# Other start addresses in SBUF for the weight buffers and for the arrays that stream past them

## The chip, the cores and the metric

The kernel runs on one core of one Trainium2 chip. The metric is device time in microseconds (us) of one execution; a kernel's time is the median of its runs.

## The reference

A first block (rms norm, one wide projection, chunked attention with relative bias, a short convolution, two gated branches, a mixture of 32 experts in 4 groups, a gated per-token embedding), then a second block of two layers on 512 tokens and 16 meta tokens: a pooling mixer and a SwiGLU FFN in layer 0, sliding-window attention and a SwiGLU FFN in layer 1.

```python
z = n @ w_in[i] + b_in[i]
...
m = jax.nn.sigmoid(ga) * (ya @ w_pa[i]) + jax.nn.sigmoid(gc) * (yc @ w_pc[i])
h = h + m @ w_o[i]
...
hdn = jax.nn.silu(xb @ w1[e]) * (xb @ w3[e])
return hdn @ w2[e]
...
gate = jax.nn.sigmoid(rms_norm(h, g_ple[i]) @ w_ple_gate[i] + b_ple_gate[i])
h = h + gate * (p[i] @ w_ple_proj[i])
...
gu = h @ w_gate_up
gate, up = jnp.split(gu, 2, axis=-1)
return (jax.nn.silu(gate) * up) @ w_down
```

All data are float32, D = 1024, S = 512 tokens, L = 528 with the meta tokens, and the FFN is 2816 wide.

## The kernel before

Activations lie transposed: 128 features on the partitions, tokens along the free axis, one row per block of 128 features. Every dense product outside the experts is made of three matmuls in float32r, since each operand is held as a high and a low part: high weights on high data, high weights on low data, low weights on high data. The helper `tile` (its matmul is L484) makes one output block: for each of the K blocks of 128 input features it issues, for each range of tokens, the three matmuls into one PSUM bank. The weights are the stationary operand (128 by 128); the tokens' row is the moving one and streams past them:

```python
for o, c0, c1 in outs:
    for n, (a, x) in enumerate(((wh, hi), (wh, lo), (wl, hi))):
        i = e.matmul(o, a, x[:, k0 + k, c0:c1], start=(k == 0 and n == 0),
                     stop=(k == j.K - 1 and n == 2))
```

Each matmul has a weight load (LDWEIGHTS, the row PEld) of its own. Of S-wide arrays (xhi, mhi, yahi, ychi, n1hi, g1hi, qhi and their low parts) a row is 512 tokens, streamed whole or in halves of 256. Of L-wide ones (nhi, nlo, ghi, glo, all of layer 0) a row is 528 tokens, streamed as 272 and 256. L1134 and L878 are the same three matmuls written out for the openings of the two FFNs, where several output blocks take turns with each row; L540 makes the values of the first attention with x as the stationary operand and the weights streamed.

Weights come in units of 8 blocks, 128 x 1024 in float32. SP loads a unit into one of four `raw` buffers, ScalarE casts it into a high part `whi` (L2319), VectorE takes the difference as the low part `wlo` (L1318), and PE waits for it by the event "lo". There are four places for such pairs (0 to 3), and four more (4 to 7) and again four (8 to 11, named wh8 to wh11 and wl8 to wl11) in stretches where room is free. `wslot(u)` names the place of unit u.

The experts (L700 up, L724 down, L735 and L736 to spread the result over the tokens) use plain float32 weights out of ten slots `e0` to `e9` of 16 KB per partition, which SP loads one after another from about 350 to 850 us.

The addresses are set by hand: a `Place` hands out addresses one after another, rounded to 32 bytes, and may be started anywhere. `keep` holds what lives throughout; behind it stand three regions of 49152 bytes, EB (raw, whi, wlo), EA and EC (activations), and XR. The function `like_weights(o)` (L303) raises an address until it has the weights' residue modulo 256; it sets n1hi, n1lo, g1hi, g1lo, and osum, qhi, qlo. The order of the work is the order in which each engine's program is written; addresses have no part in it.

Of the kernel before, what the change touches and what calls it, by code (L numbers as in the profile page):

```python
# [7 lines left out]
F32R = mybir.dt.float32r  # L8
# [6 lines left out]
S = 512  # L15
MT = 16
L = S + MT
# [121 lines left out]
def build_program(nc, T, out, known):  # L139
    with ExitStack() as ctx:  # L140
        marks = Marks(nc, ctx, known)
        _program(nc, ctx, T, out, marks)
        return marks.now


def _program(nc, ctx, T, out, marks):
# [5 lines left out]
    class Place:  # L152
# [3 lines left out]
        def __call__(self, name, shape, dt=F32):  # L156
            t = nc.alloc_sbuf_tensor_at(name, shape, dt, offset=self.off)
            self.off += (4 * int(np.prod(shape[1:])) + 31) // 32 * 32
            return t

    keep = Place(nc.sbuf_base)
    hT = keep("hT", [128, 8, L])
    cst = keep("cst", [128, NCST])
# [14 lines left out]
    ove = keep("ove", [128, 16], I32)  # L178
    wr = Place(dg_at)("wr", [128, 8, 36])
    rr = Place(dg_at)("rr", [128, 2, 3, 68])  # L180
    EB, EA, EC = keep.off, keep.off + 49152, keep.off + 98304
    XR = keep.off + 147456
    ident, ones, tri = cst[:, 0:128], cst[:, 128:256], cst[:, 256:384]
    half, tokid = cst[:, 384:512], cst[:, 512:516]

    pl = Place(EB)
# [9 lines left out]
    pl = Place(EA)  # L196
# [8 lines left out]
    pl = Place(EC)  # L205
# [3 lines left out]
    yalo = pl("yalo", [128, 4, S], F32R)  # L209
    pl = Place(XR)  # L210
    ychi = pl("ychi", [128, 4, S], F32R)
# [4 lines left out]
    Bt.append(pl("B1", [128, 2, S]))  # L216
    pl = Place(XR)
    mhi = pl("mhi", [128, 8, S], F32R)
    mlo = pl("mlo", [128, 8, S], F32R)
    sg = pl("sg", [128, 2, S])  # L220

    LAST = (nc.sbuf_usable_end - 16384) // 32 * 32
    slots = [Place(o + 16384 * i)(f"e{c}", [128, 4096]) for c, (o, i) in enumerate(
        ((EA, 1), (EA, 2), (EA, 0), (EC, 0), (EC, 1), (EC, 2), (EB, 0), (EB, 1), (EB, 2), (LAST, 0)))]
    WIDE = 50
# [20 lines left out]

    pl = Place(XR)
    xg = [pl("xg0", [128, D])]
    pl.off = XR + 4160
    xg.append(pl("xg1", [128, D]))  # L250
# [7 lines left out]
    pick = pl("pick", [128, S], F32R)  # L258
    assert pl.off <= LAST
    pl = Place(XR)  # L260
    pick_last = pl("pick15", [128, S], F32R)
    h2 += [pl(f"h2{i}", [128, 4, C]) for i in (2, 3)]
    assert pl.off <= XR + 4160

# [16 lines left out]
    pl = Place(EB + 8192)  # L281
    pThi = pl("pThi", [128, 2, S], F32R)
    pTlo = pl("pTlo", [128, 2, S], F32R)
    pl = Place(XR)
# [3 lines left out]
    pl = Place(EA)  # L288
# [2 lines left out]
    zacc = pl("zacc", [128, L])  # L291
    zq = [pl(f"zq{i}", [128, 272]) for i in range(5)]
    tmp = [pl(f"ztmp{i}", [128, 272]) for i in range(3)]
    y_at = pl.off
    yT = pl("yT", [128, 8, L])
    f_at = pl.off
    ghi = pl("ghi", [128, 12, L], F32R)
    glo = pl("glo", [128, 12, L], F32R)
    sl = [pl(f"sl{i}", [128, L]) for i in range(2)]
    gdiag = pl("gdiag", [128, 8, 128])  # L300
    assert pl.off <= nc.sbuf_usable_end

    def like_weights(o):  # L303
        return o + (EB - o) % 256

    n1hi = Place(like_weights(EA))("n1hi", [128, 8, S], F32R)
    n1lo = Place(like_weights(EA + 32 * L))("n1lo", [128, 8, S], F32R)
    g1hi = Place(like_weights(f_at))("g1hi", [128, 12, S], F32R)
    g1lo = Place(like_weights(f_at + 48 * L))("g1lo", [128, 12, S], F32R)
    assert like_weights(EA + 32 * L) + 32 * S <= EA + 64 * L  # L310
    assert like_weights(f_at + 48 * L) + 48 * S <= f_at + 96 * L
    assert like_weights(f_at) + 48 * S <= f_at + 48 * L
    ho = Place(EA)("ho", [128, 4, D])
    XW = 4
    whi += [None] * 8
# [1 line left out]
    pl = Place(f_at)  # L317
# [6 lines left out]
    plo = [None, pl("plo1", [128, 8, 256], F32R)]  # L324
    pl.off = max(pl.off, (LAST - 13824) // 32 * 32)
    assert pl.off >= f_at + 96 * L + 8 * L
    zn = pl("zn", [128, 8, MT + 272])
    ws = [pl(f"ws{i}", [128, 2, 14 + 272]) for i in range(2)]
    assert pl.off <= LAST
    pl = Place(LAST)  # L330
    pp = [pl(f"pp{i}", [128, 8, 256]) for i in range(2)]
    pl = Place(y_at)
    phi[0] = pl("phi0", [128, 8, 256], F32R)
    plo[0] = pl("plo0", [128, 8, 256], F32R)
    for n, (x, o) in enumerate(((whi, f_at + 4 * 4 * L), (wlo, f_at + 16 * 4 * L))):
        pl = Place(o)
# [4 lines left out]
    pl = Place(f_at)  # L341
# [3 lines left out]
    B2 = [pl(f"B2{i}", [128, 4, 256]) for i in range(2)]  # L345
    PT2 = [pl(f"PT2{i}", [128, 4, 128]) for i in range(2)]
    sm = pl("sm", [128, 5, 64])
    pl.off = like_weights(pl.off + 32 * S)
    osum = Place(pl.off)("osum", [128, 8, S])
    qhi = pl("qhi", [128, 8, S], F32R)  # L350
    qlo = pl("qlo", [128, 8, S], F32R)
# [2971 lines left out]
```

## Time and profile before

| | us |
|---|---|
| median of 3 runs | 1949.69 |
| all runs | 1949.5, 1949.69, 1953.39 |
| profiled execution, its time and its span | 1949.5 |
| PE busy | 1888.2 |
| VectorE busy | 917.4 |
| ScalarE busy | 637.3 |
| GpSimd busy | 139.6 |

The profile is of one execution, the one of 1949.5 us. PE's busy time is made of modelled ends, and successive matmuls overlap in it: a matmul's own duration in a row (some 0.39 us for 512 columns) holds the way through the array, and the time from one start to the next is what a stream of them costs. DMA moves 345.16 MB in the span.

### The profile page before, as it was taken

Reading aid. Unit: us, or ns where it says so; the run is one execution under the profiler, and the core shown is the slowest. Engines: PE = TensorE matmul, PEld = TensorE weight load, DVE = VectorE, ACT = ScalarE, POOL = GpSimd, SP = SyncE. Lnnn points to the kernel's source line nnn. Section 1 sums busy time; section 2 is a strip of 40 time slices with the busy share of each in tenths; the row PEclk is TensorE's granted clock in tenths of the full one; section 3 lists DMA queues with packets and bytes.
Section 4 is the critical chain, followed back from the end, with each engine's and each line's share of the span. In section 5 each row is a group of like instructions: output and inputs, shape, how many; then the busy total and the mean of one; then the engine's idle time right before and its main releaser. Section 6 shows DMA issues by size and latency. Waiting matters only on the chain.

```text
span 1949.5 us, 31374 instructions
## 1 busy us (share of the span) xinstructions
PE 1888.2 (97%) x13564; PEld 1563.9 (80%) x13564; DVE 917.4 (47%) x1611; ACT 637.3 (33%) x1187; POOL 139.6 (7%) x120
## 2 busy tenths in 40 slices
PE   7999999999999999999899999999999999999998
PEld 5866788866666666669789999999867898888898
DVE  5755334233332333247873322347866574423355
ACT  6344323121111011126532222234466543222242
POOL 0022000110000000000000000004222100000011
PEclk9999999999999999999899999999999999999999
DMA  5222242689999999973112332334321213332343
GB/s 190 87 76 76 86 170 94 267 348 427 425 425 426 423 427 424 426 291 91 47 61 83 91 98 78 96 104 144 111 66 55 79 53 108 94 110 82 104 126 112
DMA packets 57149, 345.16 MB, mean 177 GB/s; under 512 B 7168, under 2 KB 7808, under 8 KB 44976
## 3 DMA queue, kind: packets, MB, share of 16 engines
q1 hardware_dynamic: 53184, 334.15, 46.4%
q0 software_dynamic: 3504, 8.54, 1.3%
q8 instruction: 108, 1.77, 0.4%
q10 hardware_dynamic: 320, 0.43, 0.1%
q14 instruction: 33, 0.27, 0.0%
HBM read 343.09 MB, written 4.19 MB: 178 GB/s over the span
## 4 chain that ended last, share of the span: by engine, by line
PE 84%; DVE 7%; DMA 6%; ACT 1%; issue 1%; POOL 0%; SPq 0%; DVEq 0%; ACTq 0%; POOLq 0%
PE bank L484 57%; PE bank L700 8%; PE bank L724 6%; DMA e<-in_we 6%; PE bank L735 1%; PE bank L540 1%; PE bank L736 1%; DVE wlo L1318 1%; PE bank L1134 1%; PE bank L1081 1%; PE bank L917 1%; PE bank L1053 1%; PE bank L878 1%; PE bank L687 1%; PE bank L557 1%
## 5 line engine op out<-in xcount | busy, mean ns | idle before, releaser
L1318 DVE TENSOR_TENSOR wlo<-raw,whi 128x1024 fp32r<-128x1024 f32 x230 | 286.6, 1253 | 127.3 <-ACT whi L2319 123.3
L2319 ACT CAST whi<-raw 128x1024 fp32r<-128x1024 f32 x231 | 239.8, 1043 | 127.3 <-PE bank L484 110.3
L700 PE MATMUL bank<-e,xT 128*64 128x256 f32 x2048 | 234.7, 382 | 1.0 <-DVE xT L1591 1.0
L700 PEld LDWEIGHTS bank<-e,xT 128*64 128x64 f32 x2048 | 143.0, 137 | 80.5 <-issue 11.2
L484 PE MATMUL bank<-nhi,whi 128*128 128x272 f32 (+1 forms) x672 | 191.6, 285 | 1.1 <-DVE sl L1847 0.6
L484 PE MATMUL bank<-nhi,wlo 128*128 128x272 f32 (+1 forms) x672 | 191.2, 285 | 0.0
L484 PE MATMUL bank<-nlo,whi 128*128 128x272 f32 (+1 forms) x672 | 190.6, 284 | 0.0
L484 PE MATMUL bank<-n1hi,whi 128*128 128x512 f32 (+1 forms) x448 | 163.0, 364 | 0.0
L484 PE MATMUL bank<-n1hi,wlo 128*128 128x512 f32 (+1 forms) x448 | 160.8, 359 | 0.0
L484 PE MATMUL bank<-n1lo,whi 128*128 128x512 f32 (+1 forms) x448 | 160.8, 359 | 0.0
L724 PE MATMUL bank<-e,h 128*64 128x256 f32 x1024 | 118.7, 392 | 11.7 <-DMA e<-in_we 11.2
L484 PEld LDWEIGHTS bank<-nhi,whi 128*128 128x128 f32 x672 | 127.2, 189 | 2.0 <-DVE sl L1847 0.8
L484 PEld LDWEIGHTS bank<-nlo,whi 128*128 128x128 f32 x672 | 126.8, 189 | 0.0
L484 PEld LDWEIGHTS bank<-nhi,wlo 128*128 128x128 f32 x672 | 126.3, 188 | 0.0
L1618 DVE SCALAR_TENSOR_TENSOR ylo<-bank,tcol,yhi 128x512 fp32r<-128x512 f32 x32 | 24.0, 751 | 211.4 <-ACT yhi L2500 211.4
L484 PE MATMUL bank<-xhi,whi 128*128 128x512 f32 x288 | 121.2, 421 | 1.3 <-DVE xlo L1342 1.3
L724 PEld LDWEIGHTS bank<-e,h 128*64 128x64 f32 x1024 | 79.2, 141 | 49.2 <-issue 15.3
L484 PE MATMUL bank<-xhi,wlo 128*128 128x512 f32 x288 | 112.8, 392 | 0.0
L484 PE MATMUL bank<-xlo,whi 128*128 128x512 f32 x288 | 112.5, 391 | 0.0
L484 PE MATMUL bank<-ghi,whi 128*128 128x272 f32 (+1 forms) x352 | 101.3, 288 | 2.8 <-DVE wlo L1318 2.7
L484 PE MATMUL bank<-ghi,wlo 128*128 128x272 f32 (+1 forms) x352 | 100.7, 286 | 0.0
L484 PE MATMUL bank<-glo,whi 128*128 128x272 f32 (+1 forms) x352 | 100.5, 285 | 0.0
(397 smaller groups left out, 3762.9 us busy)
## 6 DMA issues: line engine op xcount, KB each, us to landing
e<-in_we SPq DMA_DIRECT2D x94, 2048.0 KB, 22.6
raw<-in_w_down SPq DMA_DIRECT2D x64, 512.0 KB, 3.6
raw<-in_w_gate SPq DMA_DIRECT2D x44, 512.0 KB, 3.6
raw<-in_w_up SPq DMA_DIRECT2D x44, 512.0 KB, 3.6
raw<-in_w_q SPq DMA_DIRECT2D x12, 512.0 KB, 4.5
B<-in_rel POOLq DMA_DIRECT2D x8, 512.0 KB, 4.7
raw<-in_w_gc SPq DMA_DIRECT2D x8, 512.0 KB, 3.5
raw<-in_w_ga SPq DMA_DIRECT2D x8, 512.0 KB, 4.3
```

Of the source, the lines that this page charges most:

```text
L484: i = e.matmul(o, a, x[:, k0 + k, c0:c1], start=(k == 0 and n == 0), stop=(k == j.K - 1 and n == 2))
L540: p = e.matmul(bs[i][:, 0:256], x[:, k, t], a, start=(k == 0 and n == 0), stop=(k == 7 and n == 2))
L557: e.matmul(b[:, 0:n], qk[pb:pb + 64, hp, t * 128:(t + 1) * 128], qk[pb:pb + 64, 4 + hp, 0:n], start=True, stop=True).then_inc(*hit("pe_att ...
L687: i = e.transpose(b[:, k * 128:(k + 1) * 128], xg[0 if ov else p % 2][:, (4 * c + k) * 128:(4 * c + k + 1) * 128], ident)
L700: p = e.matmul(b[64 * hf:64 * hf + 64, 0:256], x[:, k, :], W[:, k, 256 * hf:256 * hf + 256], start=(k == 0), stop=(k == 7))
L724: i = e.matmul(b[64 * x:64 * x + 64, 256 * q:256 * q + 256], h2_of(2 * p + x)[:, 2 * (kc % 2) + kc // 2, :], W[x][:, kc, 512 * nh + 256 * ...
L735: e.matmul(b[:], yhi[:, k * 128:(k + 1) * 128], pick_of(p)[:], start=True, stop=False)
L736: e.matmul(b[:], ylo[:, k * 128:(k + 1) * 128], pick_of(p)[:], start=False, stop=True).then_inc(*hit(f"pe_moe{ov}", ("spread y", p, k)))
L878: p = e.matmul(o, a, x[:, k, c0:c1], start=(k == 0 and n == 0), stop=(k == 7 and n == 2))
L1318: e.tensor_tensor(wlo[wslot(u)][:], raw[u % NRAW][:], whi[wslot(u)][:].bitcast(F32), ALU.subtract).then_inc(*hit("dve_low", ("lo", u)))
L1618: e.scalar_tensor_tensor(ylo[:, c], bk("y", p, nh), tcol[:, 1, p:p + 1], yhi[:, c].bitcast(F32), ALU.mult, ALU.subtract).then_inc(*hit(f"d ...
L2319: e.copy(whi[wslot(u)][:], raw[u % NRAW][:]).then_inc(*hit("act_high", ("hi", u)))
```

## The change

Only addresses change. EB is put 64 bytes past a multiple of 256, EA and with it EC and XR at multiples of 256; `like_weights` gives way to `whole`, which rounds up to 256; the last slot `LAST`, yT and what starts there are put at multiples of 256, and f_at (ghi, glo, and the places 4 to 11) 64 past one. No instruction, wait or transfer is added, dropped or moved to another point of its engine's order.

The residues modulo 256 that come out, with the relation, which is the stationary operand's start less the moving one's, modulo 256:

| stationary / streamed | before | relation | after | relation |
|---|---|---|---|---|
| places 0 to 3 / xhi, mhi, yahi, ychi, n1hi, g1hi, qhi and low parts | 96 / 96 | 0 | 64 / 0 | 64 |
| places 0 to 3 / pThi, pTlo | 96 / 96 | 0 | 64 / 64 | 0 |
| places 0 to 3 / phi0, plo0 | 96 / 160 | 192 | 64 / 0 | 64 |
| places 0 to 3 / phi1, plo1 | 96 / 160 | 192 | 64 / 64 | 0 |
| places 4 to 7 / phi0, plo0 | 160 / 160 | 0 | 64 / 0 | 64 |
| places 4 to 7 / phi1, plo1 | 160 / 160 | 0 | 64 / 64 | 0 |
| places 8 to 11 / n1hi, n1lo | 160 / 96 | 64 | 64 / 0 | 64 |
| xhi, xlo / places 0 to 3 (L540) | 96 / 96 | 0 | 0 / 64 | 192 |
| yhi, ylo / pick (L735, L736) | 160 / 160 | 0 | 64 / 64 | 0 |
| places 0 to 3 / rows of nhi, ghi | 96 / 32, 96, 160, 224 | all four | 64 / 0, 64, 128, 192 | all four |
| experts' slots e0 to e8; e9 (DMA targets) | 96; 224 | | 0 or 64; 0 | |

```diff
--- before.py
+++ after.py
@@ -157,6 +157,9 @@
             t = nc.alloc_sbuf_tensor_at(name, shape, dt, offset=self.off)
             self.off += (4 * int(np.prod(shape[1:])) + 31) // 32 * 32
             return t
+
+    def whole(o):
+        return (o + 255) // 256 * 256
 
     keep = Place(nc.sbuf_base)
     hT = keep("hT", [128, 8, L])
@@ -178,8 +181,9 @@
     ove = keep("ove", [128, 16], I32)
     wr = Place(dg_at)("wr", [128, 8, 36])
     rr = Place(dg_at)("rr", [128, 2, 3, 68])
-    EB, EA, EC = keep.off, keep.off + 49152, keep.off + 98304
-    XR = keep.off + 147456
+    EB = whole(keep.off) + 64
+    EA = whole(EB + 49152)
+    EC, XR = EA + 49152, EA + 98304
     ident, ones, tri = cst[:, 0:128], cst[:, 128:256], cst[:, 256:384]
     half, tokid = cst[:, 384:512], cst[:, 512:516]
 
@@ -219,7 +223,7 @@
     mlo = pl("mlo", [128, 8, S], F32R)
     sg = pl("sg", [128, 2, S])
 
-    LAST = (nc.sbuf_usable_end - 16384) // 32 * 32
+    LAST = (nc.sbuf_usable_end - 16384) // 256 * 256
     slots = [Place(o + 16384 * i)(f"e{c}", [128, 4096]) for c, (o, i) in enumerate(
         ((EA, 1), (EA, 2), (EA, 0), (EC, 0), (EC, 1), (EC, 2), (EB, 0), (EB, 1), (EB, 2), (LAST, 0)))]
     WIDE = 50
@@ -291,25 +295,22 @@
     zacc = pl("zacc", [128, L])
     zq = [pl(f"zq{i}", [128, 272]) for i in range(5)]
     tmp = [pl(f"ztmp{i}", [128, 272]) for i in range(3)]
-    y_at = pl.off
+    y_at = pl.off = whole(pl.off)
     yT = pl("yT", [128, 8, L])
-    f_at = pl.off
+    f_at = pl.off = whole(pl.off) + 64
     ghi = pl("ghi", [128, 12, L], F32R)
     glo = pl("glo", [128, 12, L], F32R)
     sl = [pl(f"sl{i}", [128, L]) for i in range(2)]
     gdiag = pl("gdiag", [128, 8, 128])
     assert pl.off <= nc.sbuf_usable_end
 
-    def like_weights(o):
-        return o + (EB - o) % 256
-
-    n1hi = Place(like_weights(EA))("n1hi", [128, 8, S], F32R)
-    n1lo = Place(like_weights(EA + 32 * L))("n1lo", [128, 8, S], F32R)
-    g1hi = Place(like_weights(f_at))("g1hi", [128, 12, S], F32R)
-    g1lo = Place(like_weights(f_at + 48 * L))("g1lo", [128, 12, S], F32R)
-    assert like_weights(EA + 32 * L) + 32 * S <= EA + 64 * L
-    assert like_weights(f_at + 48 * L) + 48 * S <= f_at + 96 * L
-    assert like_weights(f_at) + 48 * S <= f_at + 48 * L
+    n1hi = Place(whole(EA))("n1hi", [128, 8, S], F32R)
+    n1lo = Place(whole(EA + 32 * L))("n1lo", [128, 8, S], F32R)
+    g1hi = Place(whole(f_at))("g1hi", [128, 12, S], F32R)
+    g1lo = Place(whole(f_at + 48 * L))("g1lo", [128, 12, S], F32R)
+    assert whole(EA + 32 * L) + 32 * S <= EA + 64 * L
+    assert whole(f_at + 48 * L) + 48 * S <= f_at + 96 * L
+    assert whole(f_at) + 48 * S <= f_at + 48 * L
     ho = Place(EA)("ho", [128, 4, D])
     XW = 4
     whi += [None] * 8
@@ -345,7 +346,7 @@
     B2 = [pl(f"B2{i}", [128, 4, 256]) for i in range(2)]
     PT2 = [pl(f"PT2{i}", [128, 4, 128]) for i in range(2)]
     sm = pl("sm", [128, 5, 64])
-    pl.off = like_weights(pl.off + 32 * S)
+    pl.off = whole(pl.off + 32 * S)
     osum = Place(pl.off)("osum", [128, 8, S])
     qhi = pl("qhi", [128, 8, S], F32R)
     qlo = pl("qlo", [128, 8, S], F32R)
```

## Rows read from the trace of the kernel before

**Rows 1.** The page: span, busy time by engine, TensorE's clock in 40 slices.

```profile
span 1949.5 us, 31374 instructions
...
PE 1888.2 (97%) x13564; PEld 1563.9 (80%) x13564; DVE 917.4 (47%) x1611; ACT 637.3 (33%) x1187; POOL 139.6 (7%) x120
...
PEclk9999999999999999999899999999999999999999
```

**Rows 2.** The page: the chain that ended last, by line.

```profile
PE bank L484 57%; PE bank L700 8%; PE bank L724 6%; DMA e<-in_we 6%; PE bank L735 1%; PE bank L540 1%; PE bank L736 1%; DVE wlo L1318 1%; PE bank L1134 1%; PE bank L1081 1%; PE bank L917 1%; PE bank L1053 1%; PE bank L878 1%; PE bank L687 1%; PE bank L557 1%
```

**Rows 3.** The longest of PE's waits: total us, times, longest us.

```profile
PE bank L724 <- DMA e<-in_we: 11.2, 5, 4.3
```

**Rows 4.** Window 350 to 850 us: busy by engine, PEclk, DMA share, GB/s.

```profile
350.00:850.00 500.00, 483.47 (x3757) 329.49 (x3758) 155.59 (x300) 64.39 (x131) 25.88 (x24) 0.98 0.97 403
```

**Rows 5.** Timeline of PE from 1660 us (start, us, what), first and last.

```profile
1659.66 0.39 PE L484 MATMUL bank<-n1hi,wlo 128*128 128x512 f32 x1
...
1661.47 0.39 PE L484 MATMUL bank<-n1lo,whi 128*128 128x512 f32 x1
```

**Rows 6.** Timeline of PE from 1545 us, first and last.

```profile
1545.43 0.28 PE L484 MATMUL bank<-n1hi,whi 128*128 128x256 f32 x1
...
1546.39 0.28 PE L484 MATMUL bank<-n1hi,wlo 128*128 128x256 f32 x1
```

**Rows 7.** Timeline of PE from 1598 us, places 8 to 11 at L484.

```profile
1597.83 0.28 PE L484 MATMUL bank<-n1hi,wl 128*128 128x256 f32 x1
...
1598.96 0.28 PE L484 MATMUL bank<-n1hi,wh 128*128 128x256 f32 x1
```

**Rows 8.** Timeline of PE, from 1566 us, L1134, places 8 to 10.

```profile
1565.73 0.28 PE L1134 MATMUL bank<-n1lo,wh 128*128 128x256 f32 x1
...
1567.14 0.28 PE L1134 MATMUL bank<-n1lo,wh 128*128 128x256 f32 x1
```

**Rows 9.** Timeline of PE from 918 us, phi1 with places 0 to 3.

```profile
918.43 0.28 PE L484 MATMUL bank<-plo,whi 128*128 128x256 f32 x1
...
919.84 0.28 PE L484 MATMUL bank<-plo,whi 128*128 128x256 f32 x1
```

**Rows 10.** Lines by form, PE: first products of 512 columns at L484.

```profile
L484 PE MATMUL bank<-n1hi,whi 128*128 128x512 f32 x320 | 125.8, 393 | 0.0
...
L484 PE MATMUL bank<-xhi,whi 128*128 128x512 f32 x288 | 121.2, 421 | 1.3 <-DVE xlo L1342 1.3
...
L484 PE MATMUL bank<-g1hi,whi 128*128 128x512 f32 x96 | 37.3, 389 | 0.0
...
L484 PE MATMUL bank<-pThi,whi 128*128 128x512 f32 x16 | 6.7, 417 | 0.0
```

**Rows 11.** Lines by form, PE: first products, 256; L-wide ones (page).

```profile
L484 PE MATMUL bank<-g1hi,whi 128*128 128x256 f32 x160 | 46.2, 289 | 0.0
...
L484 PE MATMUL bank<-phi,whi 128*128 128x256 f32 x128 | 37.9, 296 | 0.0
...
L484 PE MATMUL bank<-n1hi,whi 128*128 128x256 f32 x128 | 37.3, 291 | 0.0
...
L484 PE MATMUL bank<-nhi,whi 128*128 128x272 f32 (+1 forms) x672 | 191.6, 285 | 1.1 <-DVE sl L1847 0.6
...
L484 PE MATMUL bank<-ghi,whi 128*128 128x272 f32 (+1 forms) x352 | 101.3, 288 | 2.8 <-DVE wlo L1318 2.7
```

**Rows 12.** Windows of PE: length, busy (matmuls), PEclk, DMA share, GB/s.

```profile
1030.00:1100.00 70.00, 70.00 (x579) 1.00 0.30 91
1640.00:1700.00 60.00, 60.00 (x266) 1.00 0.33 103
```

**Rows 13.** The page: the split of a weight unit on DVE.

```profile
L1318 DVE TENSOR_TENSOR wlo<-raw,whi 128x1024 fp32r<-128x1024 f32 x230 | 286.6, 1253 | 127.3 <-ACT whi L2319 123.3
```

**Rows 14.** Timeline of PE from 353.8 us, on mhi.

```profile
353.89 0.40 PE L484 MATMUL bank<-mhi,wlo 128*128 128x512 f32 x1
...
355.05 0.39 PE L484 MATMUL bank<-mlo,whi 128*128 128x512 f32 x1
```

## The prediction

> **What bounds the kernel now.** The page first. Its span is 1949.5 us, and TensorE (PE) is busy for 1888.2 us of it with the granted clock at 9 tenths or more in all 40 slices but one; VectorE has 917.4 us and ScalarE 637.3 us [rows 1]. In the chain that ended last the one matmul line L484 holds 57% of the span [rows 2]. The waits say the same from the other side: the most that PE spends on anybody is 11.2 us, on the experts' weights [rows 3]. So outside the experts' stage PE never stands still, and what a matmul takes from its own start to the next one's start is the price that counts. Inside that stage the 16 DMA engines are 97% busy [rows 4]; there a faster matmul buys nothing.
>
> The profiled execution (1949.5 us) is the lowest of the three runs and 0.2 us under their median of 1949.69, so sums against it hold for the median.
>
> **How long a matmul really takes.** The column "mean ns of one" holds the pipeline's latency, so I read starts in the timeline. A 512-column matmul on n1hi, n1lo: 1659.66 to 1661.47 is 8 steps, 226 ns each [rows 5]. At 2.4 GHz (PEclk is 1.00 there [rows 12], the higher of its two levels) 512 columns stream in 213.3 ns, so about 13 ns are lost. A 256-column one on the same arrays: 1545.43 to 1546.39, 8 steps, 120 ns against 106.7 for the columns, again 13.3 lost [rows 6]. Whatever the width, the same loss: 32 column times per matmul. In both, the weights' place and the streamed row begin at the same residue, 96 of 256 (the table of residues above).
>
> The kernel before has two places where they do not. At the second half of the last FFN's opening the weights stand in places 8 to 11 (residue 160) while n1 is at 96: weights 64 bytes ahead, which is the relation that the change gives to nearly all S-wide arrays. At L484 the steps there are 1597.83 to 1598.96, 10 of them, 113 ns: 6.6 lost, half of what it was [rows 7]. At L1134, where three places take turns, 1565.73 to 1567.14 is 12 steps of 117.5 ns: 10.8 lost [rows 8]. Weights 64 bytes behind, phi1 at 160 and places 0 to 3 at 96, give 1.41 us for 12 steps, 117.5 ns [rows 9]. So the relation matters, by 2.2 to 6.7 ns a matmul, and equal residues are the worst of the three seen.
>
> **The change, term by term.** No instruction, wait or queue entry is added, dropped or moved; only addresses are. So the sum is a count times a difference in step.
>
> 1. 512-column matmuls at L484 whose relation goes from 0 to 64. There are eight groups of first products there, from n1hi's 320, xhi's 288 and g1hi's 96 down to pThi's 16, 912 in all [rows 10]; each has two sister groups of equal count (the low part streamed, the low part as weights), so 2736. The pThi group stays at relation 0 (64 and 64), which takes off 48: 2688. No row shows 512 columns at relation 64. The loss at relation 0 is the same 13 ns for both widths, so I carry over the two values seen at 256 columns, 6.7 and 2.2 ns gained; the same relation shows both [rows 7, 8] and I take the middle, 4.5: 2688 x 4.5 = 12.1 us. Ends: 5.9 and 18.0 us.
> 2. 256-column matmuls on n1 and g1 at relation 0: (128 + 160) x 3 = 864 [rows 11], x 4.5 = 3.9 us. Ends 1.9 and 5.8.
> 3. phi (128 x 3 [rows 11]): before, half at relation 0 and half at weights-behind; after, phi0 at 64, phi1 at 0. 13.3 and 11.1 become 8.9 and 13.3: 384 x 1.1 = 0.4 us. The values' product (L540, 192 of 256 columns), where weights and stream change roles, goes from 0 to weights-behind: 192 x 2.2 = 0.4 us.
> 4. The L-wide arrays (nhi, nlo, ghi, glo; 3 x 672 + 3 x 352 matmuls [rows 11], with the 288 of layer 0's opening 3360). A row of 528 elements is 2112 bytes, 64 more than a multiple of 256, so the rows walk through all four relations, before as after. They took 70 us for 579 matmuls in the window 1030 to 1100, 120.9 ns at a mean width of 264 columns (110.0 ns), 10.9 lost [rows 12]: the average of the relations. Set at 0; it returns in the rival below.
> 5. The experts' matmuls and the spread of their result (L735, L736, relation 0 before and, but for the last pair, after) lie under the DMA stage. The loads there land at residue 0 or 64 in place of 96 or 224. Nothing in the trace varies that; set at 0, bounded by the 1% or so that 5 us of that stage is, both ways.
> 6. VectorE and ScalarE read and write the moved tiles. One unit of weights is split in 1253 ns [rows 13]; PE needs 24 x 120 = 2.88 us for a unit at 256 columns, 2.77 after. A split grown by half would still hide. Set at 0.
>
> Sum: 12.1 + 3.9 + 0.4 + 0.4 = 16.8 us; 1949.5 - 16.8 = 1932.7, say 1933 us. With terms 1 to 3 at their ends, 1941 to 1925.
>
> **A rule for full speed.** The rows above show 226 ns for 512 columns, never less [rows 5]. The Trainium skill, "TensorE: Matmul & The Clock Gate", section "Wait — 56ns, not 53.3ns?", has back-to-back matmuls at N / 2.4 GHz plus about 2.5 ns, 215.7 ns at N = 512. By that rule, if the new places reached it, the 2688 wide ones alone would give some 29 us, against the 12.1 us of my sum. No run here shows that step.
>
> **Rivals.**
> - *The odd 32 bytes cost too.* Every loss in the trace is near a multiple of 16 columns, or a third of one: 6.7, 11, 13.3. Sixteen columns of four bytes are 64 bytes, and every streamed row of before begins at 32 past a multiple of 64 (residues 32, 96, 160, 224). If memory is read by 64 bytes, each row touches one piece more than it needs, which is 16 columns or 6.7 ns, also in the L-wide arrays. After the change all begin at multiples of 64. For: no stretch in [rows 5 to 9] loses less than 6.6, whatever the relation. Against: no row has an even place to compare. Price: 2736 + 864 + 384 + 192 + 192 (L1134 and its tiles) + 3360 = 7728 matmuls x 6.7 = 51.5 us on top of the 16.8, 1881 us; should only half of it come, 1907.
> - *Nothing changes.* If the losses come from which places follow each other (three in turn at L1134, places 8 to 11), and not from residues, the new ones keep 226 and 120: 1949.5. Against it stand [rows 7, 8] beside [rows 6]: same width and arrays, 20 and 50 us later. The Trainium skill speaks for it: "SBUF — State Buffer", section "Who interferes with whom", gives PE two independent read ports, one for the moving operand and one for the weights, so their places would not meet; by that rule the time is 1949.5 us, and the 120 against 113 of this trace is hard to square with it.
> - *Slower: 512 columns fall into a worse rhythm.* The loss is a standing pattern between two streams, and a wide matmul lets the weights' load meet it elsewhere. A wide pattern worse than 226 exists: 353.89 to 355.05 on mhi is 5 steps of 232 ns [rows 14]. If relation 64 puts the 2688 wide ones there, they lose 5 ns each, 13.4 us, while terms 2 and 3 still gain 4.7: 1958 us. It decides once the wide step is more than (4.7 + 3.9) / 2688 = 3.2 ns over 226.
>
> **Chances.** About 0.2%, 3.9 us, is what a measurement of this kernel can tell from no change. My forecast 0.40; the odd 32 bytes 0.29; nothing 0.14; slower 0.17. The first two are faster: 0.69, the third is same, 0.14, the last slower, 0.17. The range takes in the forecast, most of the 64-byte case and nearly all of the slower one: 1886 to 1958 us. The forecast's own range is 1925 to 1941.
>
> **What would show it.** In the layer-1 FFN (from about 1600 us) the 512-column steps should be 220 to 225 ns and the 256-column ones 113 to 118; the window of L-wide matmuls should still hold 579 in 70 us, while some 610 (114 ns each) would show the 64-byte case. The experts' stage should keep its length and its 97%. Wide steps of 226 mean that residues are not the cause, 229 and more the slower case. No wait of PE on a split of weights should grow.

## The result, and the profile after

The changed kernel takes 1958.67 us (median of 11 runs, 1955.92 to 1961.62) against 1951.47 us for the kernel before (11 runs): a ratio of 1.0036, 95% interval 1.0028 to 1.0044, so 7 us slower (5.5 to 8.6). Forecast was 1933 us and faster. The profiled execution has a span of 1957.1 us and a time of 1959.31. In one run of `best`, the last kernel below, the clock was granted at 0.56 and the time was 3115.86 us; its ratio leaves that run out.

Line numbers are one higher after the change (L484 is L485). The page of after:

```profile
span 1957.1 us, 31374 instructions
...
PE 1900.8 (97%) x13564; PEld 1561.2 (80%) x13564; DVE 917.8 (47%) x1611; ACT 637.6 (33%) x1187; POOL 139.7 (7%) x120
...
L1319 DVE TENSOR_TENSOR wlo<-raw,whi 128x1024 fp32r<-128x1024 f32 x230 | 286.5, 1252 | 130.3 <-ACT whi L2320 126.4
```

VectorE and the split of a unit stayed as in [rows 1, 13]; PE has 12.6 us more busy time. The span grew by 7.6 us only, since PE also waits less: for the experts' weights 6.7 us in place of 11.2 [rows 3]. Where the busy time went shows in the timeline of PE, the same matmuls as in [rows 5], first and last of 9:

```profile
1659.74 0.40 PE L485 MATMUL bank<-n1hi,whi 128*128 128x512 f32 x1
...
1661.61 0.40 PE L485 MATMUL bank<-n1hi,wlo 128*128 128x512 f32 x1
```

Eight steps in 1.87 us are 234 ns (233.3 in the long run) where they were 226 (226.7 in the long run). A 256-column matmul on g1, 12 steps early and 24 steps late in the same timeline:

```profile
1886.87 0.28 PE L485 MATMUL bank<-g1lo,whi 128*128 128x256 f32 x1
...
1888.24 0.28 PE L485 MATMUL bank<-g1lo,whi 128*128 128x256 f32 x1
...
1936.36 0.28 PE L485 MATMUL bank<-g1hi,whi 128*128 128x256 f32 x1
...
1939.19 0.28 PE L485 MATMUL bank<-g1hi,whi 128*128 128x256 f32 x1
```

114 and 118 ns each where [rows 6] had 120: at one and the same relation some stretches step at 113.3 and some at 117.8, 115.7 on the average of g1 and n1. So the narrow matmuls gained what was forecast and the wide ones lost. The windows of [rows 12], length, busy (matmuls), PEclk, DMA share, GB/s:

```profile
1030.00:1100.00 70.00, 70.00 (x579) 1.00 0.31 91
1640.00:1700.00 60.00, 60.00 (x259) 1.00 0.31 97
```

259 wide matmuls in 60 us, where there were 266; the L-wide ones, 579 in 70 us, did not change by one, though all their rows went from odd multiples of 32 bytes to multiples of 64.

Priced with these steps, 2688 wide ones at 6.7 ns would be 17.9 us lost. Not all of them lose that much. Two matmuls of the kernel before, the first ones on yc and on m:

```profile
215.59 0.39 PE L484 MATMUL bank<-ychi,whi 128*128 128x512 f32 x1
...
335.27 0.39 PE L484 MATMUL bank<-mhi,whi 128*128 128x512 f32 x1
```

and the same two after the change:

```profile
216.90 0.40 PE L485 MATMUL bank<-ychi,whi 128*128 128x512 f32 x1
...
340.10 0.40 PE L485 MATMUL bank<-mhi,whi 128*128 128x512 f32 x1
```

Between the two lie 528 wide matmuls one after another, and the changed kernel falls 3.5 us further behind, 6.7 ns each. Ahead of the first lie as many, in short stretches of 8 to 24 between other work, and there it falls behind by 1.3 us only. The reason shows in the block of [rows 14], which is at relation 0. It begins with steps of 232 ns and then settles, 9 steps in 2.04 us:

```profile
356.65 0.39 PE L484 MATMUL bank<-mhi,wlo 128*128 128x512 f32 x1
...
358.69 0.40 PE L484 MATMUL bank<-mhi,wlo 128*128 128x512 f32 x1
```

So 226.7 ns is the settled step of relation 0. About the first ten steps behind an interruption take 232 there, while relation 64 has 233 to 234 from its start on. Added up over both traces, matmul by matmul, the wide ones lose 15.1 us, the narrow ones gain 3.8 and L540 0.4. That makes 10.9 us, and the result is 7. Something else gave about 4 us back, which the experiments look for.

### The profile page after: what moved, and what is told of

It reads as the page before. It is cut to its first block, busy times and chain, and to the rows that moved or that the text cites. A ratio compares the mean times of both kernels' runs of the same rounds, so it can differ in the third digit from the quotient of the medians.

```text
span 1957.1 us, 31374 instructions
## 1 busy us (share of the span) xinstructions
PE 1900.8 (97%) x13564; PEld 1561.2 (80%) x13564; DVE 917.8 (47%) x1611; ACT 637.6 (33%) x1187; POOL 139.7 (7%) x120
## 4 chain that ended last, share of the span: by engine, by line
PE 87%; DVE 6%; DMA 4%; ACT 1%; issue 1%; POOL 0%; DVEq 0%; SPq 0%; ACTq 0%; POOLq 0%
PE bank L485 58%; PE bank L701 10%; PE bank L725 5%; DMA e<-in_we 3%; PE bank L736 1%; PE bank L737 1%; PE bank L541 1%; PE bank L1135 1%; PE bank L688 1%; PE bank L1082 1%; PE bank L918 1%; DVE wlo L1319 1%; PE bank L1054 1%; PE bank L879 1%; PE bank L558 1%
## 5 line engine op out<-in xcount | busy, mean ns | idle before, releaser
L485 PE MATMUL bank<-nhi,whi 128*128 128x272 f32 (+1 forms) x672 | 191.7, 285 | 1.1 <-DVE sl L1848 0.6
L485 PE MATMUL bank<-nhi,wlo 128*128 128x272 f32 (+1 forms) x672 | 191.2, 284 | 0.0
L485 PE MATMUL bank<-nlo,whi 128*128 128x272 f32 (+1 forms) x672 | 190.6, 284 | 0.0
L485 PE MATMUL bank<-n1hi,whi 128*128 128x512 f32 (+1 forms) x448 | 164.4, 367 | 0.0
L485 PE MATMUL bank<-n1lo,whi 128*128 128x512 f32 (+1 forms) x448 | 162.2, 362 | 0.0
L485 PE MATMUL bank<-n1hi,wlo 128*128 128x512 f32 (+1 forms) x448 | 162.2, 362 | 0.0
L485 PEld LDWEIGHTS bank<-nhi,whi 128*128 128x128 f32 x672 | 127.2, 189 | 1.9 <-DVE sl L1848 0.8
L485 PEld LDWEIGHTS bank<-nlo,whi 128*128 128x128 f32 x672 | 126.8, 189 | 0.0
L485 PEld LDWEIGHTS bank<-nhi,wlo 128*128 128x128 f32 x672 | 126.3, 188 | 0.0
L485 PE MATMUL bank<-xhi,whi 128*128 128x512 f32 x288 | 122.3, 425 | 0.6 <-DVE xlo L1343 0.6
L725 PE MATMUL bank<-e,h 128*64 128x256 f32 x1024 | 115.7, 384 | 7.3 <-DMA e<-in_we 6.7
L485 PE MATMUL bank<-xlo,whi 128*128 128x512 f32 x288 | 113.8, 395 | 0.0
L485 PE MATMUL bank<-xhi,wlo 128*128 128x512 f32 x288 | 113.8, 395 | 0.0
L485 PE MATMUL bank<-ghi,whi 128*128 128x272 f32 (+1 forms) x352 | 101.3, 288 | 4.1 <-DVE wlo L1319 4.0
L485 PE MATMUL bank<-ghi,wlo 128*128 128x272 f32 (+1 forms) x352 | 100.9, 287 | 0.0
L485 PE MATMUL bank<-glo,whi 128*128 128x272 f32 (+1 forms) x352 | 100.5, 286 | 0.0
```

What stands on the lines that cost most here:

```text
L725: i = e.matmul(b[64 * x:64 * x + 64, 256 * q:256 * q + 256], h2_of(2 * p + x)[:, 2 * (kc % 2) + kc // 2, :], W[x][:, kc, 512 * nh + 256 * ...
```

## The experiments

In all of them "relation" is the weights' start less the streamed row's, modulo 256, as in the table of residues.

### A table of steps: e_even, e_odd, e_half

One kernel can hold several relations, since the weights go round four places. From the kernel before:

```diff
-    EB, EA, EC = keep.off, keep.off + 49152, keep.off + 98304
-    XR = keep.off + 147456
+    EB = (keep.off + 255) // 256 * 256 + 0
+    EA, EC, XR = EB + 49152 + 768, EB + 98304 + 768, EB + 147456 + 768
...
+    def ahead(n):
+        pl.off += (EB + n - pl.off) % 256
+        return pl
-    whi = [pl(f"whi{i}", [128, 1024], F32R) for i in range(NSP)]
+    whi = [ahead(n)(f"whi{i}", [128, 1024], F32R) for i, n in enumerate((0, 64, 128, 192))]
-    wlo = [pl(f"wlo{i}", [128, 1024], F32R) for i in range(NSP)]
+    wlo = [ahead(n)(f"wlo{i}", [128, 1024], F32R) for i, n in enumerate((0, 64, 128, 192))]
```

e_odd ends EB's line with `+ 96`; e_half has 32, 96, 160, 224 for the four places.

> The four places of weights stand 0, 64, 128 and 192 bytes past the residue of the S-wide arrays, and those begin at a multiple of 256. Theory A (only the relation weights less stream counts): 512 columns step at 226.7 ns on place 0 (relation 0), 233.3 on place 1 (relation 64), new values on places 2 and 3; 256 columns at 120.0, 113.3 to 117.8, and 117.8 on place 3. Theory B (places at odd multiples of 32 cost of themselves): place 0 steps at 220 and 113, 6.7 ns less than in the kernel before, since nothing is at an odd 32 here. Time 1945 to 1960 us.

> As e_even, everything moved by 96 bytes, so that all begin at an odd multiple of 32 as in the kernel before. Theory A: the same step as e_even on each of the four places, within 0.5 ns. Theory B: 6.7 ns more than in e_even on each. The experts' loads land at residue 96 here and at 0 in e_even: if that sets the DMA rate, e_odd moves them at 416 GB/s as before and e_even at 420; if not, both alike.

> As e_even, but the places stand 32, 96, 160 and 224 bytes past the arrays' residue. Theory A, if memory goes by whole 64-byte pieces: each pair of neighbours in relation is bounded by what e_even shows for them, no third kind of step. Theory B: the weights' loads, now at odd multiples of 32, cost 6.7 ns more than in e_even on every place. Time 1945 to 1965 us.

Measured, one run each: e_even 1952.41 us, e_odd 1964.24, e_half 1967.21, the kernel before beside them 1953.37. Single runs of one kernel differ by some us, so what tells is the timeline. In layer 1's FFN the down product streams g1 at 512 columns, 24 matmuls from each place in turn. e_even, starts at which place 1, 2, 3, 0 and again 1 begins:

```profile
1743.01 0.40 PE L490 MATMUL bank<-g1hi,whi 128*128 128x512 f32 x1
...
1748.60 0.39 PE L490 MATMUL bank<-g1hi,whi 128*128 128x512 f32 x1
...
1754.18 0.39 PE L490 MATMUL bank<-g1hi,whi 128*128 128x512 f32 x1
...
1759.69 0.39 PE L490 MATMUL bank<-g1hi,whi 128*128 128x512 f32 x1
...
1765.14 0.40 PE L490 MATMUL bank<-n1hi,whi 128*128 128x512 f32 x1
```

The differences by 24 are 232.9 ns at relation 64, 232.5 at 128, 229.6 at 192, 227.1 at 0. e_odd, the same five:

```profile
1754.69 0.40 PE L490 MATMUL bank<-g1hi,whi 128*128 128x512 f32 x1
...
1760.29 0.39 PE L490 MATMUL bank<-g1hi,whi 128*128 128x512 f32 x1
...
1765.86 0.39 PE L490 MATMUL bank<-g1hi,whi 128*128 128x512 f32 x1
...
1771.37 0.39 PE L490 MATMUL bank<-g1hi,whi 128*128 128x512 f32 x1
...
1776.82 0.40 PE L490 MATMUL bank<-n1hi,whi 128*128 128x512 f32 x1
```

233.3, 232.1, 229.6, 227.1: the same within 0.5 ns, with everything 96 bytes further on. Where an array begins counts for nothing in the steps; the relation does. The 12 us between the two kernels are elsewhere: their first matmul of the experts stands at the same time, 415.6 us, and 9.3 us of the difference arise in the experts' stage, where e_odd's loads move 425 GB/s and e_even's 429 (416 and 420 were expected). e_half, places 1, 2, 3, 0, 1 (relations 96, 160, 224, 32):

```profile
1755.97 0.39 PE L490 MATMUL bank<-g1hi,whi 128*128 128x512 f32 x1
...
1761.59 0.39 PE L490 MATMUL bank<-g1hi,whi 128*128 128x512 f32 x1
...
1767.18 0.40 PE L490 MATMUL bank<-g1hi,whi 128*128 128x512 f32 x1
...
1772.78 0.39 PE L490 MATMUL bank<-g1hi,whi 128*128 128x512 f32 x1
...
1778.38 0.39 PE L490 MATMUL bank<-n1hi,whi 128*128 128x512 f32 x1
```

234.2 at 96, 232.9 at 160, 233.3 at 224 and at 32. Theory A with whole 64-byte pieces, by which 224 would lie between 192 and 0, fails here, and with it the expectation of no third kind of step: 224 and 32, on both sides of 0, are as bad as 64. The relation counts down to 32 bytes. Theory B is out: its place 0 in e_even should have stepped at 220.

The 256-column matmuls of e_even, 12 steps each on place 3, place 2 and place 0:

```profile
1897.70 0.28 PE L490 MATMUL bank<-g1hi,whi 128*128 128x256 f32 x1
...
1899.12 0.28 PE L490 MATMUL bank<-g1hi,whi 128*128 128x256 f32 x1
...
1906.15 0.28 PE L490 MATMUL bank<-g1hi,whi 128*128 128x256 f32 x1
...
1907.57 0.28 PE L490 MATMUL bank<-g1hi,whi 128*128 128x256 f32 x1
...
1913.08 0.28 PE L490 MATMUL bank<-g1hi,whi 128*128 128x256 f32 x1
...
1914.52 0.29 PE L490 MATMUL bank<-g1hi,whi 128*128 128x256 f32 x1
```

118 ns on places 3 and 2, 120 on place 0. So the table, ns per matmul in settled stretches:

| relation | 0 | 64 | 128 | 192 | 32, 96, 160, 224 |
|---|---|---|---|---|---|
| 512 columns | 226.7 | 233.3 | 232 | 230 | 233 to 234 |
| 256 columns | 120 | 113.3 or 117.8 | 118 | 118 | |

Where two values stand, both were seen at that relation. The two widths want opposite things: 0 is the best relation for 512 columns and the worst of the four for 256.

### The change taken apart: p_even and r_odd

p_even is the kernel before with its regions moved to multiples of 256, all relations kept; r_odd is the changed kernel with the rounding moved by 96 and the last slot left at 224, so that it has the change's relations at before's odd multiples of 32.

```diff
p_even, from before:
-    EB, EA, EC = keep.off, keep.off + 49152, keep.off + 98304
-    XR = keep.off + 147456
+    EB = (keep.off + 255) // 256 * 256
+    EA, EC, XR = EB + 49152, EB + 98304, EB + 147456
-    LAST = (nc.sbuf_usable_end - 16384) // 32 * 32
+    LAST = (nc.sbuf_usable_end - 16384) // 256 * 256
r_odd, from the change:
-        return (o + 255) // 256 * 256
+        return (o - 96 + 255) // 256 * 256 + 96
-    LAST = (nc.sbuf_usable_end - 16384) // 256 * 256
+    LAST = (nc.sbuf_usable_end - 16384) // 32 * 32
```

> The kernel before with every region moved on to a multiple of 256, so that all relations stay as they were (0 for nearly all S-wide arrays) and only the odd 32 bytes go. From e_even against e_odd: the steps stay 226.7 and 120 ns, and the experts' loads take 357 us in place of 360 for the same 150 MB. Expected 1947 to 1949 against before's 1950 to 1951, a ratio of 0.9985 (0.9975 to 1.000). If the even places cost or gain elsewhere (a theory of losses by absolute place), the ratio lies outside this.

> The change with all places 96 bytes further on: its relations (weights 64 ahead), but at odd multiples of 32 as in before. 512-column steps 233.3 ns, 256-column ones 113 to 118. 2688 x 6.7 = 17.9 us lost, part of it (some 5 us, what precedes the experts' stage) taken up again by that stage's DMA bound, 4.7 us gained at 256 columns; no DMA gain. Expected 1958 to 1963, ratio 1.004 to 1.006, slower than the change by about the 3 us of the loads.

Measured: p_even 1946.35 us, ratio 0.9974 (0.9964 to 0.9984); r_odd 1962.58 us, ratio 1.0051 (1.0036 to 1.0065). The product, 1.0025, is the change's 1.0036 within the intervals. So the change is two things: relations, 10 us slower (7 to 13), which the 10.9 us added up above agree with, and even places, 5 us faster (3 to 7). For p_even that is a little more than was expected (a ratio of 0.9975 at best).

The even places gain in the experts' stage: the stage's first matmul stands at 412.2 us before and at 412.1 in p_even, its last product starts at 862.4 and at 854.8. Window 480 to 830 us, busy time by engine, PEclk, DMA share, GB/s; the kernel after, then p_even, then r_odd:

```profile
480.00:830.00 350.00, 342.94 (x2723) 223.83 (x2720) 110.06 (x187) 42.97 (x94) 10.52 (x11) 0.99 1.01 428
```

```profile
480.00:830.00 350.00, 343.50 (x2723) 224.35 (x2724) 112.32 (x190) 42.17 (x92) 9.85 (x10) 0.99 1.01 429
```

```profile
480.00:830.00 350.00, 341.28 (x2704) 223.83 (x2703) 109.36 (x184) 42.77 (x93) 10.92 (x11) 0.99 1.01 425
```

The kernel before also has 425 there. The 94 loads of 2048 KB are 197 MB: 464 us at 425 GB/s, 460 at 429, 4 us. A second, smaller piece seems to hang on it: at the stage's end PE waits longer where the loads are slower, and the clock is granted at half its rate for a moment. Window 835 to 865, kernel before, then p_even:

```profile
835.00:865.00 30.00, 26.75 (x206) 18.66 (x206) 7.70 (x13) 3.09 (x7) 0.00 (x0) 0.94 0.88 344
```

```profile
835.00:865.00 30.00, 29.48 (x232) 20.91 (x229) 13.16 (x20) 7.65 (x13) 0.00 (x0) 1.00 0.83 321
```

0.06 of 30 us is 1.8 us of clock, the most that this piece can be worth. All four kernels with odd slots (before, e_odd, r_odd, d_slots below) show 0.94 in this window, those with even ones 1.00. PE's wait for the experts' weights is 11.2 us before [rows 3] and in p_even

```profile
PE bank L724 <- DMA e<-in_we: 6.3, 2, 5.2
```

### Is it the loads' target? d_slots

p_even with eight of the ten slots 32 bytes lower, at residue 224, with gaps made for them:

```diff
-    EA, EC, XR = EB + 49152, EB + 98304, EB + 147456
+    EA, EC, XR = EB + 49408, EB + 98816, EB + 147968
-    slots = [Place(o + 16384 * i)(f"e{c}", [128, 4096]) for c, (o, i) in enumerate(
+    slots = [Place(o + 16384 * i - 32 * (c > 1))(f"e{c}", [128, 4096]) for c, (o, i) in enumerate(
```

> p_even with eight of the ten experts' slots 32 bytes lower, at residue 224, all else at multiples of 64. If an odd multiple of 32 as the loads' target costs DMA rate, 150 MB of experts' weights take 359.6 us where p_even takes 357, and the time rises by 2.5 to 4 us, ratio 0.999. If the rate hangs on something else that moved, the loads stay at 357 and the ratio at 0.997.

Measured: 1949.14 us, ratio 0.9985 (0.9976 to 0.9994). That is 2.8 us over p_even, and 2.6 over `best` below, which has even slots and ran beside it; about half of the 5 us, for eight slots of ten. Its window:

```profile
480.00:830.00 350.00, 341.15 (x2716) 224.30 (x2712) 109.36 (x184) 42.16 (x92) 9.85 (x10) 1.00 1.01 426
```

426 GB/s and an 11.2 us wait, with every other array at a multiple of 64. The target's odd 32 bytes slow the loads. All traces fall in two groups: 425 or 426 GB/s with odd slots (before, e_odd, r_odd, d_slots), 428 or 429 with even ones. The Trainium skill, "SBUF — State Buffer", section "Door 1: The DMA port swizzle (why `[64,N]` ≈ `[32,N]`)", has a port carry 32-byte transactions; by that alone a multiple of 32 would be as good as one of 64, and the runs differ from it by 0.8%.

### Where the loss passes: late64 and early64

late64 is p_even with the relation 64 in layer 1 alone; early64 is the change with layer 1's streamed arrays moved up to relation 0.

```diff
late64, from p_even:
-    n1hi = Place(like_weights(EA))("n1hi", [128, 8, S], F32R)
+    n1hi = Place(like_weights(EA) + 192)("n1hi", [128, 8, S], F32R)
...
early64, from the change:
-    n1hi = Place(whole(EA))("n1hi", [128, 8, S], F32R)
+    n1hi = Place(whole(EA) + 64)("n1hi", [128, 8, S], F32R)
...
```

and the same for n1lo, g1hi, g1lo, qhi, qlo.

> p_even with the relation 64 in layer 1 alone (n1, g1, q, streamed behind the weights by 64): 1440 matmuls of 512 columns at 233.3 in place of 226.7 are 9.6 us lost, 864 of 256 columns 3.8 us gained, nothing stands between them and the end. Expected 5.8 us over p_even, 1952, ratio 1.000. The change against p_even then has 8.3 us more of loss ahead of the experts' stage; it was 12 us over p_even, so 5 to 6 of the 8.3 should reach the end. If the loss ahead of that stage is hidden, late64 comes out as slow as the change.

> The change with layer 1's streamed arrays (n1, g1, q) moved up by 64, so that only the 1200 wide matmuls ahead of the experts' stage (x, ya, yc, m) keep the relation 64, and layer 1 has relation 0. If what is lost there reaches the end, the parts add up: ratio to before 0.9974 (even places) x 1.0062 / 1.0032 (the change over p_even, less layer 1's part from late64) = 1.0004, so 1951 to 1953 us, with 233.3 ns steps on xhi and mhi and 226.7 on n1. If the experts' stage took up the loss ahead of it, the ratio stays near 0.998 and the time near 1947.

(The wide matmuls ahead of the experts' stage are 1248, not 1200: 864 on x, 96 each on yc and ya, 192 on m.) Measured: late64 1952.95 us, ratio 1.0006 (0.9996 to 1.0016); early64 1954.55 us, ratio 1.0019 (1.0009 to 1.0029). Windows of PE from 1640 us, late64, then early64:

```profile
1640.00:1700.00 60.00, 60.00 (x259) 1.00 0.32 94
```

```profile
1640.00:1700.00 60.00, 60.00 (x267) 1.00 0.33 99
```

and in early64's timeline before the experts' stage 9 steps of 233 ns:

```profile
328.73 0.39 PE L485 MATMUL bank<-xhi,whi 128*128 128x512 f32 x1
...
330.83 0.40 PE L485 MATMUL bank<-xhi,whi 128*128 128x512 f32 x1
```

Against p_even, late64 is 6.2 us slower (5.8 expected). early64 is 8.8 us slower (1.0019 / 0.9974) where its 1248 steps of 6.7 ns make 8.3. By the traces, where the short stretches lose less, early64 reaches the experts' stage 5.8 us behind p_even, and its last product of that stage starts 7.3 us behind (862.1 against 854.8). Nothing of the loss ahead of the DMA-bound stage is taken up by it: SP issues the first of its loads at 348.0 us in early64 and at 343.4 in p_even, and resumes them at 415.8 and 410.0. The expectation of late64, 5 to 6 us of 8.3, was wrong on this; early64's, a ratio of 1.0004 if all of the loss comes through, lies under the interval. The sum of both, 15 us, is more than the 12.3 us between the change and p_even, but within the errors of four ratios of 0.1% each.

### Mixes: e_hi, e_lo, e_low

High and low parts of the weights at different relations, from e_even's layout: e_hi has 0, 64, 128, 192 for whi and 0 four times for wlo, e_lo the reverse. e_low is p_even with n1lo moved by 64, g1lo by 128, qlo by 192, nlo by 64, glo by 128 against their high parts.

> High parts of the weights at 0, 64, 128, 192 on places 0 to 3, low parts all at 0. Two loads in three are changed: 231.1, 230.6 and 228.7 ns at 512 columns by thirds; anything that is not such a mean shows that the pattern of three is one standing rhythm. A step under 226.7 would be a better mix than equal residues.

> Low parts of the weights at 0, 64, 128, 192 past the arrays' residue on places 0 to 3, high parts all at 0. If each load meets the stream that runs while it is fetched, one load in three is changed: the 512-column step should move from 226.7 by a third of what it did with all three, to 229, 228.6 and 227.7. If what counts is where a matmul's own weights stand to its own row, the same thirds but on other members of the trio. A step under 226.7 would be a better mix than equal residues.

> p_even with the low parts of the streamed arrays moved against the high ones: n1lo by 64, g1lo by 128, qlo by 192, nlo by 64, glo by 128. One stream in three meets its load at another relation. By thirds the 512-column step would be 228 to 229 on n1, g1 and q; the L-wide pairs, which walk through all relations, should keep 121 ns on average. A step under 226.7 or under 120.9 would be a better mix.

One run each: 1955.19, 1952.57 and 1958.67 us. e_hi, timeline, starts of places 1, 2, 3, 0:

```profile
1745.32 0.40 PE L490 MATMUL bank<-g1hi,whi 128*128 128x512 f32 x1
...
1750.91 0.39 PE L490 MATMUL bank<-g1hi,whi 128*128 128x512 f32 x1
...
1756.50 0.39 PE L490 MATMUL bank<-g1hi,whi 128*128 128x512 f32 x1
...
1762.04 0.39 PE L490 MATMUL bank<-g1hi,whi 128*128 128x512 f32 x1
```

232.9, 232.9 and 230.8 ns: the high parts alone bring the full loss at 64 and 128, not two thirds (231.1 expected). e_lo:

```profile
1743.04 0.39 PE L490 MATMUL bank<-g1hi,whi 128*128 128x512 f32 x1
...
1748.58 0.39 PE L490 MATMUL bank<-g1hi,whi 128*128 128x512 f32 x1
...
1754.15 0.39 PE L490 MATMUL bank<-g1hi,whi 128*128 128x512 f32 x1
...
1759.69 0.39 PE L490 MATMUL bank<-g1hi,whi 128*128 128x512 f32 x1
```

230.8, 232.1, 230.8 where 229, 228.6 and 227.7 were expected: more than a third in each, and at 128 and 192 no less than with all three. So the losses of a trio of matmuls do not add up from its members. e_low's windows:

```profile
1640.00:1700.00 60.00, 60.00 (x260) 1.00 0.32 97
1030.00:1100.00 70.00, 70.00 (x575) 1.00 0.29 88
```

Of wide ones 260 where early64 and p_even have 267, of L-wide ones 575 against 579. No mix beat equal residues at 512 columns, and none helped the L-wide arrays.

### The best of both: best

p_even with phi0, phi1 put at residue 192 and places 4 to 7 at 0, so that phi, streamed only at 256 columns, has relation 64, and places 8 to 11 left 64 ahead of n1:

```diff
-    y_at = pl.off
+    y_at = pl.off = (pl.off + 63) // 256 * 256 + 192
-    f_at = pl.off
+    f_at = pl.off = (pl.off + 255) // 256 * 256
+    pl.off += 192
     phi = [None, pl("phi1", [128, 8, 256], F32R)]
-    for n, (x, o) in enumerate(((whi, f_at + 4 * 4 * L), (wlo, f_at + 16 * 4 * L))):
+    for n, (x, o) in enumerate(((whi, f_at + 4 * 4 * L + 64), (wlo, f_at + 16 * 4 * L + 64))):
```

> p_even with the two arrays that are streamed at 256 columns alone (phi, and n1 past places 8 to 11) put or kept 64 bytes behind their weights; all that is streamed at 512 stays at relation 0, all at multiples of 64. By the table of steps phi's 384 matmuls fall from 12.2 ns lost to 9, 1.2 us. Expected 1.2 us under p_even: ratio to before 0.997 (0.996 to 0.998). It may not be told apart from p_even; if phi's stage is paced by VectorE and not by PE, nothing is gained.

Measured: 1946.51 us, ratio 0.9974 (0.9964 to 0.9984), not to be told from p_even's 1946.35. The 1.2 us stay below what the measurement can tell. Both beat the kernel before by 5 us, and p_even is the simpler.

## Why the prediction was wrong

- **Term 1 failed, by its sign.** "The loss at relation 0 is the same 13 ns for both widths, so I carry over the two values seen at 256 columns": the equality at relation 0 says nothing about relation 64. There 256 columns lose 6.6 to 11 ns and 512 columns 20. Forecast: 12.1 us gained; measured in the traces: 15.1 us lost (17.9 if every wide matmul had settled at 226.7 before). The prediction itself had noted that no row shows 512 columns at relation 64, and still bounded the term by 5.9 and 18.0 us of gain, without a row that excluded a loss.
- **Terms 2 and 3 held.** 113 to 118 ns on g1 and n1, as in [rows 7, 8]; L540 at weights-behind goes to 118 as [rows 9] had it. Forecast 4.7 us gained, found 4.2.
- **Term 4 held**: 579 matmuls in 70 us before and after.
- **Term 5 failed too, put at nothing.** "Nothing in the trace varies that; set at 0": the loads went from 425 to 428 or 429 GB/s, and p_even shows 5 us for the even places. It is as large as the bound of 5 us that the term was given, and the sum left it out. It lowers the time, so the two errors are of opposite sign, and the miss would be larger without it.
- **The odd 32 bytes** as a rival are refuted for TensorE: neither the L-wide rows nor e_even against e_odd show any effect of the absolute place. The 6.6 ns that no stretch undercut remain lost at multiples of 64 too. The same 32 bytes do matter, but on the DMA side, which the rival did not name.
- **The starting time.** The prediction takes 1949.5 us as time and as span of the profiled execution. In all 13 later profiles the time is 2.2 us above the span, so this span goes with a time of about 1951.7, near the 1951.47 of 11 runs; forecast and range were some 2 us low by this alone.
- **Nothing changes** is refuted as a forecast. By the two independent read ports of the Trainium skill, "SBUF — State Buffer", section "Who interferes with whom", weights and stream would not meet; in these runs their relation moves the step by 6.7 ns. Whether the ports or something behind them is shared, no run shows. The full-speed step of 215.7 ns from the Trainium skill, "TensorE: Matmul & The Clock Gate", section "Wait — 56ns, not 53.3ns?", was seen at no relation; 226.7 is the least.
- **The slower rival was the right one** in what it said of the wide steps: "512 columns fall into a worse rhythm". Its reason, that a wide matmul lets the weights' load meet the stream elsewhere, is not shown. Its row, 232 ns on mhi [rows 14], was at relation 0, in the unsettled start of a block, and says nothing of relation 64; that 233.3 came out close to it is chance. So is the time: its 1958 us start 2 us too low, have the wide loss at 13.4 us in place of 15.1 and lack the 5 us of the even places, errors that cancel. It had 0.17. The measured 1958.67 us lies just above the range.

What stays open is the cause inside the chip. The steps at 512 columns are 34 and 35 times 16 columns (226.7 and 233.3 ns), at 256 columns 17 and 18 times (113.3 and 120): 16 columns, or 64 bytes, lost two or three times per wide matmul and once or twice per narrow one. 117.8 is the mean of a trio of 120, 120 and 113.3. That the weights' load and the moving row take turns at something that repeats every 256 bytes is a guess; no run shows it, and the step at relation 224 did not come out as pieces of 64 bytes would have it. Why the two widths differ, why the same relation gives 113 or 118 ns, and why relation 0 needs some ten steps to settle at 512 columns was not found out. Nor was why a load's target counts by 64 bytes.

## What to carry to other kernels

Where float32r matmuls with a weight load each run back to back, measure the step from start to start for each width and each relation of the two operands' addresses before moving them, and do not carry a step from one width to another: here relation 0 is best for 512 columns and worst for 256, by 3% and 6% of a step. Look whether a stretch is long enough to settle; in short ones the better relation gained 2.5 ns a matmul and not 6.7. One kernel whose buffers stand at different relations gives the whole table in one profile. Where large DMA loads bound a stage, try targets at multiples of 64 bytes; here it cost nothing and gave 0.26%.

## What the hardware showed that was not expected

A target 32 bytes off a multiple of 64 lowers a saturated load stream from 429 to 425 GB/s. The start-to-start time of a matmul depends on its operands' addresses modulo 256, from 226.7 to 234 ns at 512 columns. The step of 226.7 ns is reached only after about ten matmuls at 232. A loss ahead of a DMA-bound stage was not hidden by it: the stage's first loads were issued later by about as much.
